# Sixteen attention heads divided on one engine: where the softmax division runs in a 153-unit transformer kernel

## What is computed

```python
# first block
m = jnp.maximum(jnp.max(logits, axis=-1, keepdims=True), sink)
p = jnp.exp(logits - m)
probs = p / (jnp.sum(p, axis=-1, keepdims=True) + jnp.exp(sink - m))
o = jnp.einsum('bnkgqs,bnskd->bnqkgd', probs.astype(vb.dtype), vb)
# second model, odd layer
ps = [jnp.exp(s - m) for s in logits]
denom = jnp.exp(sink - m)
for p in ps:
    denom = denom + jnp.sum(p, axis=-1, keepdims=True)
return [p / denom for p in ps]
```

## Time and profile before

| | |
|---|---|
| median of 3 executions | 2284.5 us (2276.71 to 2289.14) |
| the profiled execution, its own time | 2281.5 us |
| its span in the trace | 2279.7 us |
| PE matmuls busy | 94% of the span |
| DVE busy | 57% |
| ACT busy | 33% |
| POOL busy | 9% |
| clock granted to PE, mean | 0.962 of full speed |

### The profile page before, as it was taken

The page is one execution under the profiler, slowest core; times in us unless marked ns, Lnnn a source line. Parts: engine busy times, 40 slices in busy tenths (PEclk is TensorE's granted clock), DMA queues, the critical chain, the costliest instruction groups (busy, mean ns, idle before and its releaser), DMA issues. The chain is left out here.

```text
span 2279.7 us, 26081 instructions
## 1 busy us (share of the span) xinstructions
PE 2142.1 (94%) x10360; PEld 1753.3 (77%) x10360; DVE 1301.7 (57%) x2189; ACT 752.2 (33%) x1391; POOL 197.7 (9%) x170
## 2 busy tenths in 40 slices
PE   5989889999999999999989999798998999999896
PEld 4876668788888888888758888587877778888785
DVE  6238854673273273265478888775344436666634
ACT  4236632431131131122261212273224225445422
POOL 2003320100000000000020000000002002222201
PEclk9977989999999999999999999899999999999998
DMA  4100021231232232222121132114121121011212
GB/s 154 52 24 1 1 93 47 84 129 47 83 113 64 74 107 78 74 102 78 52 93 37 52 92 70 42 47 171 65 102 60 55 70 36 24 38 36 97 47 83
DMA packets 42872, 157.98 MB, mean 69 GB/s; under 512 B 4352, under 2 KB 9088, under 8 KB 41472
## 3 DMA queue, kind: packets, MB, share of 16 engines
q1 hardware_dynamic: 40304, 146.49, 18.9%
q10 hardware_dynamic: 2448, 9.84, 1.1%
HBM read 136.39 MB, written 19.92 MB: 69 GB/s over the span
## 5 line engine op out<-in xcount | busy, mean ns | idle before, releaser
L179 PE MATMUL banks<-u2H,wH 128*128 128x512 f32 x736 | 300.4, 408 | 13.5 <-DVE u2L L373 5.5
L180 PE MATMUL banks<-u2L,wH 128*128 128x512 f32 x736 | 290.0, 394 | 0.0
L181 PE MATMUL banks<-u2H,wL 128*128 128x512 f32 x736 | 289.5, 393 | 0.0
L179 PE MATMUL banks<-uH,wH 128*128 128x512 f32 x672 | 263.3, 392 | 1.2 <-DVE uL L375 1.2
L180 PE MATMUL banks<-uL,wH 128*128 128x512 f32 x672 | 262.9, 391 | 0.0
L181 PE MATMUL banks<-uH,wL 128*128 128x512 f32 x672 | 262.9, 391 | 0.0
L179 PE MATMUL banks<-aH,wH 128*128 128x512 f32 x640 | 249.1, 389 | 2.0 <-PEq L201 2.0
L181 PE MATMUL banks<-aH,wL 128*128 128x512 f32 x640 | 249.0, 389 | 0.0
L180 PE MATMUL banks<-aL,wH 128*128 128x512 f32 x640 | 249.0, 389 | 0.0
L174 DVE TENSOR_TENSOR wL<-raw,wH 128x1024 fp32r<-128x1024 f32 x153 | 187.8, 1229 | 102.8 <-ACT wH L169 102.7
L169 ACT CAST wH<-raw 128x1024 fp32r<-128x1024 f32 x153 | 159.7, 1045 | 226.8 <-DMA raw<-in_wstream 222.0
(11 more groups left out here) (286 smaller groups left out, 3825.9 us busy)
## 6 DMA issues: line engine op xcount, KB each, us to landing
raw<-in_wstream SPq DMA_DIRECT2D x153, 512.0 KB, 3.5
mod_w<-in_mod_w SPq DMA_DIRECT2D x48, 512.0 KB, 5.6
x_scratch<-h SPq DMA_DIRECT2D x2, 4096.0 KB, 11.3
gt<-gates_scratch SPq DMA_DIRECT2D x8, 640.0 KB, 3.9
h<-in_x SPq DMA_DIRECT2D x4, 1024.0 KB, 10.6
h<-in_x SPq DMA_DIRECT2D x1, 4096.0 KB, 13.2
h<-x_scratch SPq DMA_DIRECT2D x1, 4096.0 KB, 12.1
xo<-x_scratch SPq DMA_DIRECT2D x1, 4096.0 KB, 12.4
```

The costliest lines, as they stand in the source:

```text
L179: first = pe.matmul(out, aH, bH, start=start, stop=False)
L180: pe.matmul(out, aH, bL, start=False, stop=False)
L181: return first, pe.matmul(out, aL, bH, start=False, stop=stop)
```

## The change

In both attentions the loop over even heads on DVE becomes a loop over even heads and then over odd ones. `normed0` is still raised behind the even heads, and `normed1` now behind the odd ones, by DVE. POOL's `divide` is gone. Nothing else differs; the waits of PE are the same. The first attention:

```diff
                         dve.wait_ge(rden_ready, k + 1)
                         lo, hi = ranges(steps[k])
-                        for hs in range(0, heads, 2):
-                            src = logits[:, k % 3, hs, lo:hi]
-                            m = dve.tensor_scalar(src, src, stat[:, SUM, k % 3, hs:hs + 1], None, ALU.mult)
-                        m.then_inc(normed0, 1)
+                        for kv, normed in enumerate((normed0, normed1)):
+                            for hs in range(kv, heads, 2):
+                                src = logits[:, k % 3, hs, lo:hi]
+                                m = dve.tensor_scalar(src, src, stat[:, SUM, k % 3, hs:hs + 1], None, ALU.mult)
+                            m.then_inc(normed, 1)
...
-                    def divide(k):
-                        pool.wait_ge(rden_ready, k + 1)
-                        lo, hi = ranges(steps[k])
-                        for hs in range(1, heads, 2):
-                            src = logits[:, k % 3, hs, lo:hi]
-                            m = pool.tensor_scalar(src, src, stat[:, SUM, k % 3, hs:hs + 1], None, ALU.mult)
-                        m.then_inc(normed1, 1)
-
                     for i, slot in enumerate(plan):
-                        if slot.sums:
-                            divide(slot.k - 1)
                         if gate and finished(i) is not None:
                             out_low(pool, finished(i))
```

## The result

| | before | after |
|---|---|---|
| median, 20 executions each | 2282.87 us (2276.71 to 2289.23) | 2289.95 us (2279.48 to 2299.55) |
| span of the profiled execution | 2279.7 us | 2283.4 us |
| its mean clock of PE | 0.962 | 0.964 |

The ratio is 1.0027, with an interval of 1.0016 to 1.0038: slower by a quarter of a percent, within the half percent that was called "same", and 7.1 us between the medians where 7.0 had been forecast (6.2 between the means, which the ratio follows). The two samples of 12 executions that followed gave 1.0024 and 1.0022. Each against the kernel before measured beside it, the three samples' means are 6.2, 5.6 and 4.6 us higher, 5.6 over all 44 executions; by the spread of the executions, a 95% interval estimated from it is 3.6 to 7.6 us.

A forecast was written before the change was run, and what follows sets the result against it. The first attention's loop through division and low part was taken as the bound, the second hidden by PE: 6.3 + 1.4 - 0.7 = +7.0 us on 2281.5, plus 3.0 to the median, gives 2291.5 us; range 2282 to 2304.

The forecast's parts named there:

- The bound: First attention: loop of division, low part, weighing, ACT and back; second attention: PE never idle, so DVE's 6 us are hidden.
- Quick steps: First attention's steps of 9.6 to 9.9 us between reciprocals, forecast to take 10.1 us after the change.
- The price of a division: First attention, DVE: 0.27 us for each division of 256 columns once POOL is gone, with bounds 0.20 and 0.49.
- Rival B: Divisions stay dear because rows are written in place: +1.9 us a step, 2312 us; chance 0.04 together with the drain.
- the drain: Milder form of B, next operation waits for empty pipeline: 0.35 us a division, 2.82 a step, 2303 us; together 0.04.
- The step: Full step of the first attention: eight divisions take 2.14 us for four's 1.69, so low parts start 0.45 us later.
- The two short steps: First attention: eight divisions of 128 columns take 1.60 us in place of 0.92, 1.4 us for both steps.
- The slow steps, counted in full: First attention's steps of 11 to 13 us also pay 0.45 each, within 14 x 0.45 = 6.3 us.
- rival C: Faster: shorter single gaps keep PE's clock up everywhere in the first attention, -16 + 7 = -9, 2276 us; chance 0.08.
- Rival A: Slower: PE's longer idle time turns three or four quick steps of the first attention slow, +9, 2300 us; chance 0.24.
- Rival D: No change: PE's transposes 0.6 us earlier close the first attention's loop, the 0.45 vanishes, 2284.5 us; chance 0.12.

The follow-up runs named there:

- twelve products: Four more products by 1.0 on DVE, behind a wait, ahead of the eight divisions of the first-attention-only kernel; 2311.12 us, ratio 1.0124 to the kernel before.

## Why the prediction was right, and where it was not

**The bound.** Right. The first attention is a loop that passes through the division and the low part behind it; the second one is covered by PE. Quick steps of 9.18 us with the same work in another order, and of 11.00 with more of it, show the loop; 274.1 us from first to last reciprocal in every kernel where it was read, and a ratio of 1.0000, show the cover.

**The price of a division.** Right: 0.27 us was forecast, (2.19 - 0.35) / 7 = 0.26 measured; durations of 353 and 547 ns forecast, medians of 349 and 548 measured. Rival B is out, and so is the drain as the prediction took it from the Trainium skill ("VectorE: DVE Perf Modes", section "The DRAIN you can't avoid"), by which eight would have taken 2.8 us. The same section says that a next operation which nothing holds starts earlier, a clause that the prediction passed over, and with it the 0.26 us agrees.

**The step.** Right: 0.44 us longer, for 0.45 forecast. The two short steps took 6.94 and 8.12 us for 6.33 and 7.44, together 1.3 for 1.4.

**The slow steps, counted in full.** Right in the mean, as far as the runs can tell, and here the closeness of 7.1 to 7.0 owes something to chance. The forecast added up 14 steps and the short ones and took off 0.7 us for steps in which PE comes late by itself; no run shows that term. From quick and short steps alone, the stretch between the reciprocals would grow by 13 x 0.44 + 1.3 = 7.0 us, and the three profiles of the changed kernel show -0.6, +8.4 and -1.6 against the first one of before. The slow steps of before add 15.9 and 18.7 us; those of the changed kernel 154.3 - 15.1 - 130.9 = 8.3, then 17.3 and 7.3. Against the 17.3 us that is the mean of before, the clock gave back nothing in one execution and 9 to 10 us in the two others, more than the loop had cost.

These five profiles are not the rule, though. The mean clock over the changed kernel's 44 executions is 0.9615, and over the 44 of before beside its second and third sample it is 0.9612: the same. The profiled executions of the changed kernel had 0.964, 0.961 and 0.966, those of before 0.962 and 0.957. So it is not shown that the change gives back any clock, and the 5.6 us over all executions (3.6 to 7.6) agree with the 7.0 of the steps.

One reading behind the rivals was wrong: the prediction took six slow steps for steps at a low clock, and the first of them, 11.22 us, had a clock of 0.99. Five were the clock's, and 1.6 of rival C's 16 us could never have come back from it.

**Rival A** did not come: its condition did, its effect is not seen. PE's idle time at a step's start grew from 1.40 to 1.70 us (1.8 forecast), and yet the profiles show 3, 7 and 3 slow steps in place of 6 and 7, each about as dear as before (2.8, 2.6 and 2.7 us over a quick one in the mean, against 2.6 and 2.9). What A rested on, that more idle time means more slow steps, is not refuted in general (twelve products: 8 of 13; none but the first with waits of 0.77 us or of 0.92 to 0.95), but between 1.4 and 1.8 us the runs don't follow it. **Rival C**, a clock that holds, did not decide the change. By the prediction's own sign for it, a mean clock above 0.85 in the first attention, it had the third profile (0.87), not the first (0.847) and not the second (0.79). It came in full only with the experiments that shortened the step. **Rival D** is out by the step's 10.07 us.

**What stays open:** why steps of 9.01 and 9.18 us never turn slow behind the first one, while of those of 9.63 us about every second does and of those of 10.07 two to six of twelve. A shorter wait of PE and a shorter step came together in every fast kernel, and no run changed the clock by itself. That the time gained beyond the steps is the clock's is read from the slow steps and the granted clock, not from such a run.

## What to carry to other kernels

Before work is moved between two engines, measure what each pays while the other works: here 0.63 of the 1.69 us that four divisions took on DVE came from POOL, so that all heads on DVE cost 0.44 us a step and not 1.9. Letting POOL start some 1.2 us later was worth more than either placement. What counts is not an engine's load but what stands ahead of the operation that another engine waits for: the same eight divisions made the kernel faster than before once the awaited low part went between them. And where PE's clock swings, a shorter step can bring twice its own gain (19 us here for 8 of the steps), and a longer one may not show in a single profile at all: compare steps at equal clock before judging an edit by one execution, and look at where in the span two profiles differ.

## What the runs showed of the hardware

- DVE and POOL, both multiplying rows in SBUF by a column, slow each other, POOL hardly: a DVE operation of 256 columns takes 0.35 us without POOL at work and 0.53 to 0.57 with it; POOL's four take 3.82 us beside DVE's divisions and 3.64 beside its other work. The Trainium skill, "SBUF — State Buffer", section "Who interferes with whom", tells of a port pair that the one holds for a whole instruction while the other is blocked. That the two collide agrees. That one is blocked for the other's whole instruction does not: POOL's four fill the time from 251.24 on, 3.82 / 4 = 0.96 us each in the mean, and DVE begins operations at 251.45, 251.94 and 252.39 and ends each in about 0.55 us.
- DVE's low parts and maxima, which read PSUM, did not change with POOL at work: 1.28 us for two low parts in a row beside POOL's divisions and without them in the changed kernel.
- A DVE product by a constant is cheaper than one by a column of values: four of 256 columns take 0.90 us together, 0.29 each and 0.20 apart, where the divisions take 0.35 each and begin 0.26 apart.
- The clock of PE falls from 1.00 to 0.50 (2.4 to 1.2 GHz) within some steps of the first attention. From 188 to 192 us before, and from 262 to 266 us in the changed kernel, it is 0.50 throughout. A step of the changed kernel then takes up to 3.5 us more, and a profiled execution of it has anything from 3 to 7 slow ones of 13. The same code spreads over 20 us, where the kernel before spread over 12.5.
